# Another deal of token rows to partitions, and two semaphores of their own, in a decoder step with routed experts

## What is computed

```
expert = g_star[:, None] * EXPERTS_PER_GROUP + top_i          # two experts per token
w_top = softmax(top_v) * p_sel                                # and their weights
for each expert e:  act = silu(h @ w_eg[e]) * (h @ w_eu[e]);  out_e = act @ w_ed[e]
x = x + sum over the token's two experts of w * out_e         # 1024 columns, float32
y = x * rsqrt(mean(x * x) + EPS) * norm_final
```

## Time and profile before

| | us |
|---|---|
| median of 3 runs (805.64 to 808.15) | 806.15 |
| the profiled execution | 805.87 |
| its span, first to last instruction | 804.0 |

### The profile page before, as it was taken

The page is one execution under the profiler, slowest core; times in us unless marked ns, Lnnn a source line. Parts: engine busy times, 40 slices in busy tenths (PEclk is TensorE's granted clock), DMA queues, the critical chain, the costliest instruction groups (busy, mean ns, idle before and its releaser), DMA issues.

```text
span 804.0 us, 12356 instructions
## 1 busy us (share of the span) xinstructions
PE 723.4 (90%) x5112; PEld 538.4 (67%) x5112; DVE 340.9 (42%) x623; ACT 244.1 (30%) x489; POOL 82.9 (10%) x138
## 2 busy tenths in 40 slices
PE   5999999999999999999999999999988787878830
PEld 4888997678999998879999978864433232233310
DVE  6643358655546347343455523732223111111128
ACT  6234374643545333333122241311110010010013
POOL 3404000000000201000000011211112111111200
PEclk9999999999999999999999999999999899999975
DMA  8732111114221713432232299679999999999935
GB/s 315 225 106 62 54 53 53 54 53 136 63 65 53 280 63 144 171 89 83 74 85 93 91 355 386 239 261 398 416 419 418 419 415 404 415 411 419 401 146 220
DMA packets 82631, 173.02 MB, mean 215 GB/s; under 512 B 8064, under 2 KB 42208, under 8 KB 82560
## 3 DMA queue, kind: packets, MB, share of 16 engines
q1 hardware_dynamic: 72736, 148.52, 49.7%
q0 software_dynamic: 9840, 23.72, 7.9%
HBM read 163.26 MB, written 18.74 MB: 226 GB/s over the span
## 4 chain that ended last, share of the span: by engine, by line
PE 66%; DMA 11%; SPq 10%; DVE 8%; ACT 2%; issue 2%; POOLq 0%; ACTq 0%; DVEq 0%
PE bank L737 44%; DMA expert_down<-in_w_exp_down 9%; SPq L544 7%; PE bank L1189 5%; PE bank L1205 4%; SPq L549 2%; DVE w_split L1548 2%; ACT w_split L1243 1%; PE bank L757 1%; PE bank L1128 1%; PE bank L1114 1%; PE bank L1022 1%; PE bank L1028 1%; DVE s_state L1846 1%; DMA token_out<-token_out_scratch 1%
## 5 line engine op out<-in xcount | busy, mean ns | idle before, releaser
L737 PE MATMUL bank<-hT_split,w_split 128*128 128x272 f32 x1152 | 154.1, 292 | 0.0
L737 PEld LDWEIGHTS bank<-hT_split,w_split 128*128 128x128 f32 x1152 | 147.3, 188 | 2.1 <-issue 0.9
L737 PE MATMUL bank<-w_split,hT_split 128*128 128x512 f32 (+1 forms) x576 | 130.1, 380 | 0.5 <-DVE w_split L1548 0.5
L1189 PE MATMUL bank<-expert_gate_up,gatheredT 128*64 128x512 f32 x512 | 113.3, 593 | 3.7 <-DMA expert_gate_up<-in_w_exp_up 2.8
L737 PEld LDWEIGHTS bank<-w_split,hT_split 128*128 128x128 f32 x576 | 100.1, 188 | 22.9 <-issue 3.3
L1548 DVE TENSOR_TENSOR w_split<-w_raw,w_split 128x2048 fp32r<-128x2048 f32 (+1 forms) x35 | 75.9, 2168 | 83.1 <-ACT w_split L1243 83.1
L1205 PE MATMUL bank<-expert_down,expert_actT 128*64 128x512 f32 x256 | 69.6, 694 | 30.9 <-DMA expert_down<-in_w_exp_down 27.5
L1189 PEld LDWEIGHTS bank<-expert_gate_up,gatheredT 128*64 128x64 f32 x512 | 38.8, 137 | 75.0 <-issue 69.5
L1243 ACT ACTIVATE w_split<-w_raw 128x2048 fp32r<-128x2048 f32 (+1 forms) x35 | 63.4, 1812 | 42.4 <-PE bank L737 17.5
L1205 PEld LDWEIGHTS bank<-expert_down,expert_actT 128*64 128x64 f32 x256 | 20.9, 156 | 68.6 <-issue 38.7
L737 PE MATMUL bank<-gla_outT_split,w_split 128*128 128x272 f32 x384 | 49.4, 288 | 0.0
(11 more groups left out here) (355 smaller groups left out, 838.6 us busy)
## 6 DMA issues: line engine op xcount, KB each, us to landing
expert_gate_up<-in_w_exp_gate SPq DMA_DIRECT2D x64, 512.0 KB, 14.7
expert_gate_up<-in_w_exp_up SPq DMA_DIRECT2D x64, 512.0 KB, 15.7
expert_down<-in_w_exp_down SPq DMA_DIRECT2D x32, 1024.0 KB, 17.0
w_raw<-in_w_in SPq DMA_DIRECT2D x15, 1024.0 KB, 5.5
w_raw<-in_w_in SPq DMA_DIRECT2D x16, 512.0 KB, 4.7
s_state<-in_state_gla POOLq DMA_DIRECT2D x4, 1024.0 KB, 8.7
out_sample_gla_state<-s_state POOLq DMA_DIRECT2D x4, 1024.0 KB, 6.3
w_raw<-in_w_proj_gla SPq DMA_DIRECT2D x8, 512.0 KB, 4.2
```

The lines of the kernel that those rows point to most:

```text
L737: ins = mm(out, stat(x, k), mov(y, k), start=first and n == 0 and m == 0, stop=last and n == len(ks) - 1 and m == 2)
L1189: ins = mm(P[2 + u][64 * half:64 * half + 64, :].rearrange("p (m n) -> p m n", m=2), XT[u][:, k, 64 * half:64 * half + 64], WGU[gb][:, k / ...
```

## The change

Two things. The constant `slot_row` is filled otherwise: partitions are seen as groups of eight, eight groups to a half. Rank 0 goes to the first partition of group 0, rank 1 to the first of group 1, and so on to rank 7 in group 7; rank 8 goes to the second partition of group 7, rank 9 to that of group 6, and so on back to group 0; and on to and fro. And the first expert's loads of blocks 0 and 1 add to semaphores of their own, `first_in`, so that DVE's first addition of these blocks waits for that load alone and the second addition for the other.

```
-SPREAD, UNSPREAD = 39, 23
...
-    assert (SPREAD * UNSPREAD) % CAP == 1
-    parts["slot_row"] = np.broadcast_to(CAP * (p // CAP) + UNSPREAD * p % CAP, (128, 128))
+    group, lap = p % CAP // 8, p % 8
+    parts["slot_row"] = np.broadcast_to(CAP * (p // CAP) + 8 * lap + np.where(lap % 2, 7 - group, group), (128, 128))
...
+        first_in = [sem("first_in0"), sem("first_in1")]
...
+                    landed = first_in[bl] if k == 0 and bl < 2 else x_in[bl]
                     sp.dma_start(YI[2 * bl + k][0:rows(bl), :],
-                                 tok_d[k * NTOK + bl * 128:k * NTOK + bl * 128 + rows(bl), :]).then_inc(x_in[bl], 16)
+                                 tok_d[k * NTOK + bl * 128:k * NTOK + bl * 128 + rows(bl), :]).then_inc(landed, 16)
...
-                dve.wait_ge(x_in[bl], 16 + 32)
+                if bl < 2:
+                    dve.wait_ge(first_in[bl], 16)
+                else:
+                    dve.wait_ge(x_in[bl], 16 + 32)
                 link(V.scalar_tensor_tensor(out=y1[0:n, :], in0=y1[0:n, :], scalar=R1["w1"][0:n, bl:bl + 1], in1=X2[0:n, bl, :],
                                             op0=ALU.mult, op1=ALU.add))
+                if bl < 2:
+                    dve.wait_ge(x_in[bl], 16 + 16)
                 V.scalar_tensor_tensor(out=y1[0:n, :], in0=y2[0:n, :], scalar=R1["w2"][0:n, bl:bl + 1], in1=y1[0:n, :],
                                        op0=ALU.mult, op1=ALU.add).then_inc(x3_ready, 1)
```

## The result

The changed kernel took 823.25 us (median; 820.39 to 825.58), the kernel before, measured beside it, 805.89 us. The ratio is 1.0208, with a 95% interval of 1.0170 to 1.0246: slower by 17 us. The prediction was 816.9 us, with a range of 812.5 to 820.5. The direction was right and so was the kind of loss, but it is 17.4 us by the medians (16.8 by the ratio) and not 10.7, and the measured time lies above the range.

What follows compares the result with a forecast made beforehand. The busiest DMA engine was taken to end the expert stage. Deal +11.5, first gather +0.2, last scatter +0.3 and semaphores -1.3 gave +10.7 on 805.87 us; with 0.28 for the median, 816.9 us, range 812.5 to 820.5.

Steps and rivals of the forecast that it cites:

- What bounds the kernel: Expert stage: DMA engines are full from 553 to 760 us, so the stage ends when the busiest engine ends.
- the 28 DMAs: Gathers and scatters of token rows at 553 to 760 us, taken as scatters of pairs 0-14 and gathers of pairs 3-15.
- Which grouping: Which partitions share a DMA engine: fours favoured over eights, from the stream's graded tail and the packet order.
- fours: Grouping in which an engine serves four partitions in a row and the four that lie 32 further on.
- by eights: Grouping in which an engine serves eight partitions in a row; the change would level its busiest from 149 rows to 123.
- Rivals 1 and 2: Deal: engines serve eights, 802.0 us, chance 0.08; or rows go to any free engine, deal does nothing, 804.9 us, 0.04.
- Price of the deal: Full stretch of the expert stage: busiest engine gets 214 instead of 137 rows, 0.156 us each; +11.5 us taken.
- The first gather: Before PE's transposes: busiest engine goes from 6 to 8 rows, +0.3 if all is felt, 0 if covered; +0.2 us taken.
- The last scatter: On the path after the expert stage: 8 rows on one engine instead of 6, +0.3 us, 3.2 us issue to landing.
- PE's clock: PE's granted clock around its waits for weights: no term in the sum; the upper bound counts 1.7 us for it.
- The semaphores: DVE's additions at the end: the first of a block waits only for its first load; -1.3 us, bounds -0.9 and -1.4.
- Rival 3: Half the deal's price is absorbed, as loaded engines run dry or light ones speed them up: 811.4 us, chance 0.08.

Runs made afterwards that it cites:

- e5: New semaphores, but a deal that loads a single DMA engine (211 rows on the busiest) and levels the others: ratio 1.0149 to the kernel before.
- e12: Changed kernel with half of TensorE's work in the expert stage left out: 823.36 us, ratio 1.0213 to the kernel before.
- e9: Deal of the kernel before, new semaphores, `expert_down` loads of pairs 2 to 13 issued from ScalarE's queue: 801.72 us, ratio 0.9954.
- e10: Changed kernel with `expert_down` loads of pairs 2 to 13 issued from ScalarE's queue: 820.63 us, ratio 1.0178 to the kernel before.
- e3: Changed kernel, but dealt to and fro level over partitions sharing an engine by fours (123 rows on the busiest): 805.17 us, ratio 0.9987.
- e4: Changed kernel's deal at half dose: eight loaded engines get three of four of each expert's first 32 ranks; 810.87 us, ratio 1.0050.
- e8: The changed kernel measured again, on the chip of e5 to e7: ratio 1.0218 to the kernel before, +18.9 us over e2.
- e2: The new semaphores alone, with the deal of the kernel before: 805.02 us, ratio 0.9984 to the kernel before.
- e7: Changed kernel's deal at three quarters of the dose: eight loaded engines get seven of eight of the first 32 ranks; 817.1 us, ratio 1.0138.
- e6: New semaphores, lower 64 partitions dealt level by fours, upper 64 as in the changed kernel, loading four engines: 820.4 us, ratio 1.0184.
- e14: Changed kernel with another eight engines loaded, the first four of each half instead of every other one: 823.18 us, ratio 1.0223.
- e1: The new deal alone, with the semaphores of the kernel before: 826.93 us, ratio 1.0229 to the kernel before.
- e13: Deal of the kernel before, new semaphores, half of TensorE's work in the expert stage left out: 801.99 us, ratio 0.9954.
- e11: Level deal by fours, new semaphores, `expert_down` loads of pairs 2 to 13 issued from ScalarE's queue: 801.55 us, ratio 0.9952.

## Why the prediction was right in its direction and missed the size

*What bounds the kernel* held in the main. The busiest DMA engine ends the expert stage: e5 shows it by itself, and e12 shows that with the new deal PE's work does not. It is not all, for the second queue gives 2.4 and 3.2 us (e9, e10), and e3, with fewer rows on the busiest engine, gives none. One reading was off: the 28 DMAs of 553 to 760 us are not quite those named. The scatter of pair 14 comes after 760 us, and one of the 28 is a gather for a seventeenth pair that moves no row. The rows up to the last landing are the same, so the price does not change. And the chain runs on PE up to 579 us only from 523 us on; from 517 to 522 us it goes over DVE's router steps.

*Which grouping* held: fours. The end of the weight stream stands at 0.5, as forecast, and e3 (level by fours, 216 rows on an engine by eights) costs nothing. (By fours the engines have 137, 134, 127, 125, 125 rows before; the prediction has 127 twice.) Three traces show it for the indirect DMAs of this kernel. e5 puts its extra rows on partitions 0 to 3 and 32 to 35 alone, which by eights lie on two engines, and at the end one engine is alone, with a share of 0.06 to 0.09 from 774 to 782 us. The last scatter runs by itself and moves 79 rows. By fours the changed deal puts 8 of them on each of eight engines and 1 to 3 on each of the others; by eights every engine has 4 to 6. In the changed kernel the DMA share is 0.92 from 792.3 to 792.7 us and 0.50 from there to 793.6: eight engines worked on alone. In e3, with 4 to 6 rows on every engine by fours, it is 0.97 from 774.2 to 775.0 us and 0.22 to 775.2, with no stretch at half. How a plain load lies on the partitions no run shows. That it gives each engine about the same, as the prediction's reading of the tail takes it, agrees with e3: level in rows (112 to 123 an engine), its sixteen engines go from a share of 1.02 (762 to 763 us) to 0.00 (767 to 768 us) within 4 us, after more than 200 us of full engines. Rivals 1 and 2 (802.0 and 804.9 us) are out.

*Price of the deal*: this step failed. It said +11.5, with bounds of +8.3 and +13.7. The last weight landed 17.0 us later. The price of a row, 0.156 us, was right where it could be tested alone (the 79 packets of 4,096 bytes of the last scatter took 156 to 161 ns each before, counted from the trace): e4 paid 5.3 us for a priced 5.5, e5 13.3 for 12.4. Another choice within the step would not have saved it: even the upper bound, which counts every gather and scatter, falls short. What the step did not hold is a loss beyond the rows when many engines are loaded at once, 4 to 6 us in e8. It took the busiest engine to carry its packets without a gap and at one pace, whatever the other fifteen do.

The packets in the trace, counted from 553 us to the last weight packet (no view prints this), divide the 17.0 us. The 77 rows are 12.0 us. At 553 us 181 more weight packets were still to come, eleven an engine: 1.8 us. The other 3.2 us are time of the busiest engine that its own packets at 0.1564 us do not fill, if its share of the weights is a sixteenth; since loaded engines may be behind in weights at 553 us already, some of it can be such packets. This unfilled time is 2.8 to 4.4 us with even deals (e2 2.8, before 3.5, e3 4.4), 1.6 in e4, 4.0 in e5, 5.2 in e7, 5.6 in e6, and with the full dose 6.7 in the changed kernel's first profile, 4.8 in e14, 10.3 in e1 and 10.8 in e8, the last two in traces of the slowest run. With PE half idle it is 8.1 (e12), with the second queue 6.5 (e10), where the even deals have -0.3 (e13), 0.1 (e9) and 2.1 (e11). These are single traces, and two of the same kernel differ by 4.1 us, so only the large steps count.

A part of it can be seen. From 776 to 778 us only eight engines are at work, by the count of rows the loaded ones; the share is 0.53, and they move 170 GB/s, 20 GB/s for each busy engine, where one engine moves 25 to 27 in e5. e10 from 776 to 778 us (0.55, 174 GB/s) and e12 from 778 to 780 us (0.53, 160 GB/s) have the same. In the packets, 17 weight packets that start between 776 and 779 us took more than 200 ns, up to 696, instead of 159. So loaded engines do have slow packets, though in e8's step at the end there are hardly any. Neither the queue (e10), nor PE (e12), nor the choice between two sets of eight (e14) is the cause. **What slows them stays open.**

*The first gather* was put at +0.2 and was +1.0. The prediction priced the two rows more and half covered them; the traces of e5 to e8, where the busiest engine has 8 rows like in the changed kernel, show gathers of 4.24 to 4.65 us, 0.6 to 1.0 us above e2's.

*The last scatter* was put at +0.3, 3.2 us from issue to landing: 3.29, right.

*PE's clock* has no term in the sum, and that was right. The 16 matmuls after the last landing took 3.68 us, as before. The 1.7 us that the upper bound counts for it no run shows there: these 16 took 3.67 or 3.68 us in every run with the whole of PE's work. Inside the stream they can take 5.38 us; the granted clock was 0.50 from 727 to 730 us, within those 5.38 us. The waits for `expert_down` were forecast at 39 us and were 39.5.

*The semaphores* were put at -1.3. The medians say -1.3 (e2), the traces -0.6 to -1.1, because the third load landed 0.8 us later than the row it was taken from. The size is within the term's bounds for the medians, and a little short of them in the trace.

*Rival 3* (half the price absorbed, 811.4) erred to the wrong side: nothing was absorbed, more was paid. A rival in which the loaded engines cost more than their rows was missing, and so the range ended at 820.5, below the bound of 821.3 that the prediction itself had worked out. With that bound the range would still have missed the median by 2 us.

(The middle that the prediction takes for rival 1 is 2.8 us; between 4.1 and 1.9 it would be 3.0. Nothing hangs on it.)

*Levelling* has little to give here, which the prediction did not ask. e3 is level and as fast as e2. Its engines end closer together, but from 553 to 760 us they move 414 GB/s, no more than before, where e9 moves 418. e11, with the second queue, does not gain either: ratio 0.9952 against 0.9954.

The fastest version is the old deal (or e3's) with the new semaphores and the `expert_down` loads on ScalarE's queue: 801.7 us with the old deal and 801.6 with e3's (ratios 0.9954 and 0.9952), 0.5% faster than the kernel before and 2.5% faster than the changed one.

## What to carry to other kernels

Before rows are dealt to partitions, find out which partitions share a DMA engine; a deal that is level for the wrong grouping can be very uneven for the right one, and here 77 rows of 4 KB more on the busiest engine cost 12 us by their own packets and 18 to 19 in all against e2, with the first gather and the last scatter. Count the load of the busiest engine, price it by a packet's time in a full stretch, and let the upper end of the range stand well above that when half of the engines would be loaded, for only one loaded engine, and eight at half the dose, are shown to cost their rows and little more. And read the rate beside the DMA share: the share counts a slow packet as busy, as in the changed kernel (share 1.01 at 393 GB/s, 1.03 at 415 before). A share of the DMA engines that stands at k/16 at the end of a stream says, as in the changed kernel (8, at 0.49 to 0.53) and in e5 (1, at 0.06 to 0.09), that k engines had more to do than the others.

## What was not expected of the hardware

Eight engines with 214 rows cost 18.9 us over e2, one engine with 211 rows 13.3 us, though the busiest has nearly the same work; four with up to 209 rows cost 16.1. Another set of eight (e14) and half of PE's work (e12) leave that as it is.

The first indirect gather, a DMA over 128 partitions, took 3.69 and 3.87 us with even deals (e2, e3), 3.83 with half the dose and 4.48 to 4.68 with the full dose. The last scatter took 2.92, 3.06 and 3.29 us with the even deal, half the dose and the full dose.

The DMA share stood at 1.01 while the rate fell from 415 to 393 GB/s. The counts of long weight packets (over 200 ns where nearly all take 159 ns; counted from the trace between 553 us and 768 us, no view prints them) go roughly with the loss: 106 before, 200 in e4, 445 in e5, 605 in the changed kernel and 862 in e8, of some 18,500 to 19,500. Most of them cannot be put down to an engine, and some may be those of light engines running dry; those of 776 to 779 us in the changed kernel are the loaded engines' own.
